# Ssd stage of a two-block layer: the cumulative decays of all heads reach the partitions by broadcast loads from DRAM instead of by matmuls

## What is computed

```
x    = xh * dt                                # per token and head
a_cs = cumsum(dt * A) within a chunk
decay[l, s] = exp(a_cs[l] - a_cs[s]) for l >= s, else 0      # for each head
cb   = einsum('bclgn,bcsgn->bclsg', C, B)
y_diag = einsum('bclsg,bclsgr,bcsgrp->bclgrp', cb, decay, x)
states = einsum('bclgn,bclgr,bclgrp->bcgrpn', B, exp(a_cs[end] - a_cs), x)
y_off  = einsum('bclgn,bcgrpn,bclgr->bclgrp', C, state before the chunk, exp(a_cs))
y_ssd  = rmsnorm_by_group((y_diag + y_off + d_skip * xh) * silu(z)) * gain
```

## Time and profile before

| what | us |
|---|---|
| median of 3 timed executions | 1528.99 (1525.93 to 1529.65) |
| the profiled execution, its own time | 1529.67 |
| its span, first to last instruction | 1527.8 |
| PE busy | 1368.2 |
| DVE busy | 636.0 |
| ACT busy | 377.0 |
| POOL busy | 818.6 |

### The profile page before, as it was taken

How to read it: one execution, slowest core, us unless ns; L and a number is a source line. 1 busy time by engine, 2 the same in 40 slices (tenths; PEclk the granted TensorE clock), 3 DMA queues, 4 the chain that set the end, 5 groups by cost and what they waited for, 6 DMA issues and landing times.

```text
span 1527.8 us, 18362 instructions
## 1 busy us (share of the span) xinstructions
PE 1368.2 (90%) x7156; PEld 989.5 (65%) x7156; DVE 636.0 (42%) x946; ACT 377.0 (25%) x731; POOL 818.6 (54%) x712
## 2 busy tenths in 40 slices
PE   5998979798999899999999999699997599999993
PEld 5877857676777666787788888588777233333331
DVE  2232262537890464638784566542313311111112
ACT  3211063302222475112216443231111011111110
POOL 7578723867577401878985434757950313333320
PEclk9999989999999999999999999899996699999997
DMA  5513210332214200243122111812281299999964
GB/s 197 141 56 108 72 56 7 107 119 83 83 56 138 83 1 1 83 145 102 59 81 74 53 60 61 318 42 83 83 357 56 66 369 375 372 364 362 363 244 182
DMA packets 85396, 216.30 MB, mean 142 GB/s; under 512 B 23668, under 2 KB 32580, under 8 KB 71748
## 3 DMA queue, kind: packets, MB, share of 16 engines
q1 hardware_dynamic: 62076, 199.22, 35.5%
q0 software_dynamic: 13824, 8.44, 1.9%
q10 hardware_dynamic: 9416, 7.51, 1.6%
HBM read 255.99 MB, written 26.22 MB: 185 GB/s over the span
## 4 chain that ended last, share of the span: by engine, by line
PE 45%; issue 12%; POOL 11%; PEld 10%; DVE 6%; DMA 4%; ACT 3%; POOLq 3%; DVEq 2%; PEldq 2%; ACTq 1%; SPq 0%
PE ps L1031 10%; PE ps L137 6%; PE ps L138 6%; PE ps L139 6%; POOL w_lo L504 6%; PE ps L1043 5%; POOL w_hi L501 5%; PEld ps L137 3%; PEld ps L138 3%; PEld ps L139 3%; POOLq L502 2%; PE ps L791 2%; PE ps L1023 2%; DMA w_gu<-w_up,over_u 1%; PE ps L898 1%
## 5 line engine op out<-in xcount | busy, mean ns | idle before, releaser
L501 POOL TENSOR_TENSOR w_hi<-stage,unit 128x512 fp32r<-128x512 f32 (+1 forms) x296 | 316.9, 1101 | 400.3 <-PE ps L139 388.7
L504 POOL TENSOR_TENSOR w_lo<-stage,w_hi 128x512 fp32r<-128x512 f32 (+1 forms) x296 | 396.6, 1370 | 10.5
L137 PE MATMUL ps<-hi,w_hi 128*128 128x512 f32 (+1 forms) x600 | 238.4, 397 | 19.2 <-POOL w_lo L504 9.3
L138 PE MATMUL ps<-hi,w_lo 128*128 128x512 f32 (+1 forms) x600 | 235.8, 393 | 0.0
L139 PE MATMUL ps<-lo,w_hi 128*128 128x512 f32 (+1 forms) x600 | 235.4, 392 | 0.0
L137 PE MATMUL ps<-w_hi,hi 128*128 128x512 f32 (+2 forms) x520 | 187.3, 360 | 8.7 <-ACTq L1127 2.4
L138 PE MATMUL ps<-w_hi,lo 128*128 128x512 f32 (+2 forms) x520 | 185.3, 356 | 0.0
L139 PE MATMUL ps<-w_lo,hi 128*128 128x512 f32 (+2 forms) x520 | 185.0, 356 | 0.0
L1031 PE MATMUL ps<-w_gu,xT 128*64 128x512 f32 x768 | 172.5, 602 | 3.1 <-DMA w_gu<-w_up,over_u 1.8
L137 PEld LDWEIGHTS ps<-hi,w_hi 128*128 128x128 f32 x600 | 115.0, 192 | 50.4 <-issue 15.3
L2036 DVE TENSOR_TENSOR xT<-ps,ffn_kp 128x1024 f32<-128x1024 f32 x24 | 29.4, 1224 | 250.1 <-PE ps L1023 250.1
(11 more groups left out here) (413 smaller groups left out, 1795.8 us busy)
## 6 DMA issues: line engine op xcount, KB each, us to landing
stage<-w_in SPq DMA_DIRECT2D x84, 512.0 KB, 4.5
w_gu<-w_gate SPq DMA_DIRECT2D x32, 1024.0 KB, 12.3
w_gu<-w_up SPq DMA_DIRECT2D x32, 1024.0 KB, 14.7
w_dn<-w_down SPq DMA_DIRECT2D x32, 1024.0 KB, 10.5
stage<-w_out SPq DMA_DIRECT2D x16, 512.0 KB, 4.4
stage<-w_ssd_branch SPq DMA_DIRECT2D x16, 512.0 KB, 4.7
stage<-w_in SPq DMA_DIRECT2D x20, 256.0 KB, 3.0
stage<-w_attn_branch SPq DMA_DIRECT2D x8, 512.0 KB, 4.2
```

Of the source, the lines that this page charges most:

```text
L137: pe.matmul(out, x[0], w[0], start=first, stop=False)
L138: pe.matmul(out, x[1], w[0], start=False, stop=False)
L501: nc.gpsimd.tensor_tensor(hi[:, b, k, 0:n], stage[:, b, k, 0:n], unit[:].broadcast_to([P, n]), ALU.mult)
L504: last = nc.gpsimd.tensor_tensor(lo[:, b, k, 0:n], stage[:, b, k, 0:n], hi[:, b, k, 0:n].bitcast(F32), ALU.subtract)
```

## The change

Six edits, all of them in and around the ssd stage except the last:

- The running sums of all four chunks are computed once, ahead of the first z projection, in a turn of their own: eight matmuls of 32 columns (sums along the tokens, as columns per head, and totals) and four that give the sums as rows, one partition per head. DVE copies the columns to `acs`, ACT copies the rows to `acs_rows` and stores them in DRAM (`acs_scratch`, 64 KB).
- `broadcast_rows(n)` loads the rows of 16 heads of one chunk from there to all 128 partitions, 8 KB each, 1 MB in all, into the single buffer `acs_b`. It is issued by ACT. The first is issued behind the store of `z_first`; each later one when the 16 Relus on the buffer are done. ACT's Relus read `acs_b` where they read PSUM before.
- L949 and the two small matmuls per chunk are gone from PE, and `cumulative(c)` is now `products(c)` with the `cb` part only. The exponentials of the sums are taken once for all chunks.
- DVE makes `xe` between the second and the third mask, not ahead of the first.
- The loads of the gates: `sz[0]` and `sz[1]` have places (64 and 48 KiB) which are free before the end, and SP issues them ahead of the branch's first weight tile, behind the new semaphores `btok_done` and `bT_done`; `sz[2]`, `sgb` and the rest still wait for `ssd_done`. The quarters of the gate use two buffers instead of four, and each waits for the store of two before it.
- `units()` scales the identity in one tensor_tensor over all its tiles, where it had one tensor_scalar a tile.

```diff
@@ SyncE @@
+            sp.wait_ge(btok_done, 1)
+            sp.wait_ge(gate_saved[2], 16)
+            sp.dma_start(sz[0][:], gates_dram[2]).then_inc(sz_back[0], 16)
+            sp.wait_ge(bT_done, 1)
+            for i in (3, 4):
+                sp.wait_ge(gate_saved[i], 16)
+            sp.dma_start(sz[1][:], gates_dram[3]).then_inc(sz_back[1], 16)
             halves(d["w_ssd_branch_2"][0], 0, 0)
             sp.wait_ge(ssd_done, 1)
-            for i in range(7):
+            for i in (5, 6):
                 sp.wait_ge(gate_saved[i], 16)
-            for g in range(3):
-                sp.dma_start(sz[g][:], gates_dram[2 + g]).then_inc(sz_back[g], 16)
+            sp.dma_start(sz[2][:], gates_dram[4]).then_inc(sz_back[2], 16)
...
@@ TensorE @@
+            pe.wait_ge(dt_step, 3)
+            s = turns.take()
+            for c in range(TT):
+                pe.matmul(ps[s][:, 0, 64 * c:64 * c + 32], tri[:], dts[:, 1, c, :], start=True, stop=True)
+                pe.matmul(ps[s][:, 0, 64 * c + 32:64 * c + 64], ones[:], dts[:, 1, c, :], start=True, stop=True)
+            for c in range(TT):
+                last = pe.matmul(ps[s][0:32, 1, P * c:P * (c + 1)], dts[:, 1, c, :], tri[:], start=True, stop=True)
+            last.then_inc(turn_full, 1)
             tokens()
             turn_back(6)
...
-                for half in range(2):
-                    s = turns.take()
-                    for h in range(16):
-                        col = dts[:, 1, c, 16 * half + h:16 * half + h + 1].broadcast_to([P, P])
-                        last = pe.matmul(ps[s][:, h // 4, P * (h % 4):P * (h % 4 + 1)], col, tri[:], start=True, stop=True)
-                    last.then_inc(turn_full, 1)
                 tokens(n=256)
...
@@ ScalarE @@
+            def broadcast_rows(n):
+
+                src = bass.AP(acs_dram.tensor, 16 * P * n, [[0, P], [1, 16 * P]])
+                A.dma_start(acs_b[:].rearrange("p h l -> p (h l)"), src).then_inc(acs_in, 16)
...
                     s = turns.see()
+                    A.activation(acs_rows[:], ps[s][0:32, 1, :], ACT.Copy)
+                    A.drain().then_inc(acs_copied, 1)
+                    A.dma_start(acs_dram.rearrange("c h l -> h c l"), acs_rows[:].rearrange("h (c l) -> h c l", c=TT)).then_inc(acs_saved, 16)
+                    s = turns.see()
                     A.wait_ge(mT_saved, 16)
                     A.activation(z_first[:], ps[s][:], ACT.Silu)
                     A.drain().then_inc(turn_free[s], 1)
                     A.dma_start(gates_dram[2], z_first[:]).then_inc(gate_saved[2], 16)
+                    A.wait_ge(acs_saved, 16)
+                    broadcast_rows(0)
                 rows_back(xtok[:, :, 512 * j:512 * (j + 1)])
...
                 for half in range(2):
-                    s = turns.see()
-
+                    A.wait_ge(acs_in, 16 * (2 * c + half + 1))
                     for h in range(16):
                         hh = 16 * half + h
-                        A.activation(decay[:, hh, :], ps[s][:, h // 4, P * (h % 4):P * (h % 4 + 1)], ACT.Relu,
-                                     bias=st[:, 1, k.start + hh:k.start + hh + 1], scale=-1.0)
-                    A.drain().then_inc(turn_free[s], 1)
+                        A.activation(decay[:, hh, :], acs_b[:, h, :], ACT.Relu, bias=acs[:, 0, c, hh:hh + 1], scale=-1.0)
+                    A.drain()
+                    if (c, half) != (TT - 1, 1):
+                        broadcast_rows(2 * c + half + 1)
...
@@ VectorE, units() @@
-                for t in range(n):
-                    last = V.tensor_scalar(dst[:, t, :], ident[:], st[:, 2, k + t:k + t + 1], None, ALU.mult)
-                return last
+                return V.tensor_tensor(dst[:], bc(ident[:], 1, n), bc(st[:, 2, k:k + n], 2, P), ALU.mult)
```

More of the change, by code:

```diff
@@ L145, in program @@
     x1_dram = nc.dram_tensor("x1_scratch", [S, D], F32, kind="Internal").ap()
+    acs_dram = nc.dram_tensor("acs_scratch", [TT, 32, P], F32, kind="Internal").ap()
     bias_dram = nc.dram_tensor("bias_scratch", [4, 384], F32, kind="Internal").ap()
@@ L203, in program @@
         unit_m, unit_x, unit_a = at("unit_m", 16, [P, 2, P]), at("unit_x", 17, [P, TT, P]), at("unit_a", 44, [P, TT, P])
-        unit_s = [at(f"unit_s{r}", 64 + 8 * r, [P, 2 * TT, P]) for r in range(2)]
+        unit_s = [at(f"unit_s{r}", 64 - 16 * r, [P, 2 * TT, P]) for r in range(2)]
         unit_f = at("unit_f", 20, [P, TT, P])
@@ L256, in program @@
         gate_early, gate_next = at("gate_early", 60, [P, 4, 512]), at("gate_next", 40, [P, 4, 512])
-        gate_out = [at(f"gate_out{i}", 100 + 4 * i, [P, TT, 256]) for i in range(4)]
-        sgb = at("sgb", 48, [P, KC, S])
-        sz = [at(f"sz{g}", k, [P, TT, 512]) for g, k in enumerate((64, 72, 80, 88.25))]
+        gate_out = [at(f"gate_out{i}", 100 + 4 * i, [P, TT, 256]) for i in range(2)]
+        acs_rows, acs_b = at("acs_rows", 4, [32, S]), at("acs_b", 108, [P, 16, P])
+        acs = at("acs", 116, [P, 4, TT, 32])
+        sgb = at("sgb", 72, [P, KC, S])
+        sz = [at(f"sz{g}", k, [P, TT, 512]) for g, k in enumerate((64, 48, 56, 88.25))]
         both = at("both", 64, [P, 4, 512])
@@ L325, in program @@
         gate_saved = [sem(f"gate_saved{i}") for i in range(7)]
+        acs_copied, acs_saved, acs_in = sem("acs_copied"), sem("acs_saved"), sem("acs_in")
+        btok_done, bT_done = sem("btok_done"), sem("bT_done")
         mT_half, sz_ready, gated, y_rows = sem("mT_half"), sem("sz_ready"), sem("gated"), sem("y_rows")
@@ L972, in _ @@
                     last.then_inc(turn_full, 1)
+                    if c == TT - 2:
+                        pe.drain().then_inc(btok_done, 1)
             tokens()
@@ L1318, in z_half @@
                 s = turns.see()
-                place = gate_out[(i + 2) % 4]
-                if i >= 2:
-                    A.wait_ge(gate_saved[2], 16)
+                place = gate_out[i % 2]
+                A.wait_ge(gate_saved[2 if i < 2 else 1 + i], 16)
                 A.activation(place[:], ps[s][:, :, 0:256], ACT.Silu)
@@ L1357, in _ @@
                 z_half(c)
-                turns.skip(1 + (c > 0) + 2 * (c < TT - 1))
+                turns.see()
+                turns.skip((c > 0) + 2 * (c < TT - 1))
             def squares(g):
@@ L1798, in _, with products @@
                 convolve(3 + j, 4 * j, xsT[j % 2])
-            turns.skip(11)
+            turns.skip(9)
+            s = turns.see()
+            sums = ps[s][:, 0, 0:64 * TT].rearrange("p (c k h) -> p c k h", c=TT, k=2)
+            V.tensor_copy(acs[:, 0], sums[:, :, 0, :])
+            V.tensor_copy(acs[:, 3], sums[:, :, 1, :])
+            V.wait_ge(acs_copied, 1)
+            V.drain().then_inc(turn_free[s], 1)
+            V.tensor_tensor(acs[:, 1], acs[:, 3], acs[:, 0], ALU.subtract).then_inc(acs_ready, 1)
+            turns.skip(2)
             V.wait_ge(xtok_ready, 5)
-            def cumulative(c):
-                k = slice(32 * (c % 2), 32 * (c % 2) + 32)
+            def products(c):
                 s = turns.see()
-                V.tensor_copy(st[:, 1, k], ps[s][:, 0, 0:32])
-                V.tensor_copy(st[:, 3, k], ps[s][:, 0, 32:64])
                 V.tensor_tensor(cb[:], ps[s][:, 1, :].rearrange("p (g l) -> p g l", g=4), bc(tri[:], 1, 4), ALU.mult)
                 V.drain().then_inc(turn_free[s], 1)
-                V.tensor_tensor(st[:, 2, k], st[:, 3, k], st[:, 1, k], ALU.subtract).then_inc(acs_ready, 1)
-            cumulative(0)
+            products(0)
+            V.wait_ge(e_ready, 1)
             for c in range(TT):
-                k = slice(32 * (c % 2), 32 * (c % 2) + 32)
                 V.tensor_tensor(xd[:], xtok[:, c, :].rearrange("p (h d) -> p h d", h=32), bc(dts[:, 0, c, :], 2, HD), ALU.mult)\
@@ L1817, in _ @@
                 V.drain()
[L1818 to L1820 removed]
                 for g in range(4):
[L1822 removed]
+                    if g == 2:
+                        V.tensor_tensor(xe[:], xd[:], bc(acs[:, 1, c, :], 2, HD), ALU.mult).then_inc(xe_ready, 1)
+                    V.wait_ge(e_ready, 4 * c + 2 + g)
                     m = decay[:, 8 * g:8 * g + 8, :]
                     V.tensor_tensor(m, m, bc(cb[:, g, :], 1, 8), ALU.mult).then_inc(m_ready, 1)
+                turns.skip()
                 y = xtok[:, c, :].rearrange("p (h d) -> p h d", h=32)
@@ L1832, in _ @@
                     s = turns.see()
-                    V.tensor_tensor(yoff[:], ps[s][:].rearrange("p g (h d) -> p (g h) d", d=HD), bc(st[:, 4, k], 2, HD), ALU.mult)
+                    V.tensor_tensor(yoff[:], ps[s][:].rearrange("p g (h d) -> p (g h) d", d=HD), bc(acs[:, 2, c, :], 2, HD), ALU.mult)
                     V.drain().then_inc(turn_free[s], 1)
                 if c < TT - 1:
-                    cumulative(c + 1)
+                    products(c + 1)
                     s = turns.see()
```

24 lines of the change are left out of this document (12 added, 12 removed).

## The result

The changed kernel takes **1543.62 us** (1542.98 to 1544.76), the one before in the same session 1528.6. The ratio is 1.010, interval 1.008 to 1.012: slower by 1%, where I had forecast 1523.5 with a range up to 1531. The profiled execution took 1543.88, with a span of 1542.1.

The account below looks back on a forecast made before the run. PE bounds ssd, with DVE a second chain of nearly the same length. The stage 8.1 us later, behind it 13.6 less: 1527.8 - 5.5 = 1522.3, with 1.9 around the span 1524.2, median 1523.5 us; range 1513 to 1531.

Parts of the forecast that it names:

- Chunk 0 (4.6 us later): First diagonal product starts at 839.8 against 835.2, after the new turn, store, two broadcast loads, Relus, Exps and a mask.
- Clock, 2.3 + 0 + 2.2 + 2.3 us: Time lost in chunks 0 to 3 to the lower PE clock after idling ahead of the diagonal product.
- Chunk 1 (T + 20.3): DVE's chain, the longest, sets the next diagonal product's start at T + 20.3, 5.8 us less than before.
- T: The end of a diagonal product on PE; the forecast counts from it to the start of the next one.
- Chunks 2 and 3 (T + 30.2, T + 32.6): DVE, slowed by POOL, sets the diagonal product's start: no change in chunk 2, 2.5 us more in chunk 3.
- six meetings with POOL: DVE operations slowed by POOL in each of chunks 2 and 3: 3.6 us in chunk 2, 5.7 in chunk 3.
- Behind ssd: After the ssd stage, early gates and one-operation identities end PE's wait for `unit_s`; L668 at full clock: 13.6 us less.
- The sum without the clock terms: Start of L668 from the other shifts, leaving out the clock's 2.3, 2.2 and 2.3 us; with them it was 984.3.
- Rival 3: The win behind ssd is eaten: chunk 0 or the clock takes 4 to 6 us more, 1528 to 1529; chance 0.2.
- Rival 2: Broadcast loads become the chain: slower, 1537 at 10 us a load, sign turning at about 7.3; chance 0.1.

Follow-up runs that it names:

- filler kernel: Changed kernel plus 50, 6, 36 and 46 overwritten matmuls in chunks 0 to 3, between the gate's quarter and the diagonal product: 1512.08 us, ratio 0.989.

## Why the prediction was wrong, point by point

- **Chunk 0 (4.6 us later): right to 2.1 us.** 841.9 against 839.8 (the terms as listed add up to 839.3, not 839.8), with loads of 4.8 us (4.5 assumed), a store of 4.9 us ahead of the first (3.9), and 16 Relus in 4.79 us (4.23).
- **Clock, 2.3 + 0 + 2.2 + 2.3 us: this is the step that failed.** That a wait ahead of the product lets the clock fall was right. The size was wrong: I priced it from L668, and held 2.6 us to be the most that a wait can cost. L668 brings the clock back while it runs; the diagonal product does not. It cost 6.6, 4.5, 6.6 and 6.6 us in the four products. Since the clock is still low behind them, it cost 2.2, 2.1 and 2.3 us more in the products with the state (5.83, 5.73 and 6.00 against 3.65) and some 3 us in chunk 0's two small groups. That is 34 us where I had 6.8. Filler takes it away (shown: L681 starts 32.0 us earlier), and a wait alone brings it into the kernel before (shown).
- **Chunk 1 (T + 20.3): right in the filler kernel,** where nothing is slow: 868.2 - 848.6 = 19.6. In the changed kernel it was 22. The term for the clock that I had put at nothing here, without a reason, was 4.5 us: the wait was only 1.91 us, but the clock fell inside the product behind it.
- **Chunks 2 and 3 (T + 30.2, T + 32.6): right.** The filler kernel has 905.0 - 875.6 = 29.4 and 944.4 - 912.2 = 32.1. So DVE is the second chain. The six meetings with POOL cost it 5.1 us in chunk 3 (5.7 forecast) and 2.4 us in chunk 2 (3.6 forecast), against the lengths without POOL; in the runs in which POOL starts later a pair of masks that does not meet it takes 2.36 us.
- **Behind ssd: right in kind, sized for the wrong start.** The wait for `unit_s` is gone and L681 runs at the full clock. In the kernel before these edits are worth 15 us (13 forecast). In the changed kernel they take off some 6 us, which the stage, ending 25 us later than forecast, hides in the total.
- **The sum without the clock terms** puts L668 at 977.5. The filler kernel has it at 977.18, so up to there the other terms, small misses of both signs, add up as forecast. In the changed kernel L681 starts 24.9 us later than forecast, yet the span is only 19.8 us longer than forecast. Most of the other 5 us is luck and no part of my sum: from the second turn to the end the kernel before took 484.8 us in its profiled execution and the changed one 480.4, but the kernel before with nothing but a wait added took 480.2. No edit of the change explains it.
- **The range.** An upper end of 6.6 us for each of the three clock terms would have given 1536.5, still under the measured time. Only with chunk 1's product and the groups behind the products priced too would the range have reached it.
- **Rivals.** None of the four was it. Rival 3 came nearest: it let the clock take more than forecast, but only 4 to 6 us (1528 to 1529), where it took 27 us more. Rival 2 named the slow side, but by the wrong mechanism: the loads took 4.8 us, far under the 7.3 at which it turns the sign.

The Trainium skill has the pattern ("TensorE: Matmul & The Clock Gate", section "HAM oscillation — how this bites in real kernels"): a loop of short bursts with waits between starts each burst at the lower clock. The trace agrees for the waits of 7.35 to 12.70 us. For the waits of 0.90 to 1.91 us it does not: those products start at the higher clock, and in all but one it falls inside them. The same page (Part 1) says that a short stretch of issued work restores the clock, whatever its spacing. By that, as an estimate, each product would have lost about what L668 lost, 2.6 us, near my own term. The windows of the changed kernel differ: 13.9 us of unbroken 64-column work at 0.50.

## What to carry to other kernels

Work taken off TensorE is only worth what stands next in line, and if the next in line is a wait, look at what follows it: here a group of narrow matmuls ran at the lower clock from end to end behind waits of 7 us and more, and for most of its length behind most waits of 0.9 to 1.9 us. Measure such a group at both clocks, or take its length at the lower clock as the upper bound. Place the wait ahead of wide, dense work, or fill it. Here 31.7 us of useless matmuls made the kernel 31.5 us faster, because they stood where PE waited for DVE or ACT anyway. And time each part of a change alone: two gates loaded ahead, with their new places and two semaphores, were worth 1.2% without the rest.

## What the runs showed of the hardware that I had not expected

- The diagonal product, 32 fp32 matmuls of 64 columns with a weight load each, takes 7.33 us at the granted clock 1.00 and 13.92 at 0.50, and once the clock had fallen it did not bring it back before its own end in any run here. The quarter of the projection (256 columns), L668 (128 columns) and the product with the state (512 columns, 5.83 us) did so within their own length: 14.0, 9.98 and 5.83 us. Whether the columns or the share of weight loads decide it was not tried.
- Behind short waits the clock did not fall in the wait but inside the narrow product, with PE wholly busy, 1 to 3 us after its start. It did so behind a wait of 0.90 us in one place and not behind 1.60 us in another, so the length of the wait alone does not tell. Behind 0.62 us or less no such product fell in any run here.
- ACT's Relu of 128x128 takes 4.79 us for 16 with its source in SBUF (`acs_b`) and 4.23 from PSUM, with the same output: 35 ns more for each.
- A load of the same 8 KB to all 128 partitions lands in 4.8 us for 1 MB, no slower than the ordinary load of 1 MB beside it (`sz`, 4.9).
